# Expert products of 160 tokens in plain fp32, with 32 more tokens' expert dots taken from gathered rows

## The reference, cut to what matters

```python
top, pos = lax.top_k(cand, PEER_TOPK)            # per token and head: 16 of 16384 experts
idx = jnp.take_along_axis(cand_idx, pos, axis=-1)
g = jax.nn.softmax(top.astype(jnp.float32), axis=-1)
u = u_tab[idx]                                   # u_tab, v_tab: 16384 x 2048, 128 MB each
vv = v_tab[idx]
act = jax.nn.gelu(jnp.einsum('thkd,td->thk', u, hb), approximate=False) * g
return jnp.einsum('thk,thkd->td', act, vv)       # 8 heads x 16 picks per token
```

## Time and profile before

| | us |
|---|---|
| three runs: median (lowest to highest) | 1760.01 (1758.25 to 1761.03) |
| the profiled execution, span | 1758.1 |
| UP: first matmul to last matmul | 551.15 to 1159.68 |
| DOWN: first matmul | 1162.90 |
| POOL: first put, last gather of `u_tab` | 601.37, 1138.01 |

### The profile page before, as it was taken

The page is one execution under the profiler, slowest core; times in us unless marked ns, Lnnn a source line. Parts: engine busy times, 40 slices in busy tenths (PEclk is TensorE's granted clock), DMA queues, the critical chain, the costliest instruction groups (busy, mean ns, idle before and its releaser), DMA issues.

```text
span 1758.1 us, 28277 instructions
## 1 busy us (share of the span) xinstructions
PE 1732.3 (99%) x9480; PEld 1517.9 (86%) x9480; DVE 1535.3 (87%) x2469; ACT 799.5 (45%) x1185; POOL 603.1 (34%) x413
## 2 busy tenths in 40 slices
PE   7999999999999999999999999999999999999998
PEld 5888888644999999999999999988888888888886
DVE  4668899967688898998999999989999999999997
ACT  3001222300545555556555555554455544555454
POOL 1000000011000388788688888613321211112110
PEclk9999999999999999999999999999999999999999
DMA  9999986699798777987899999999999999999994
GB/s 380 421 421 422 424 322 252 234 387 417 301 349 272 219 218 223 296 253 224 249 382 389 399 411 404 401 365 411 414 413 410 390 404 398 397 399 389 407 387 190
DMA packets 142648, 617.22 MB, mean 351 GB/s; under 512 B 45347, under 2 KB 45939, under 8 KB 87411
## 3 DMA queue, kind: packets, MB, share of 16 engines
q1 hardware_dynamic: 80530, 410.04, 60.0%
q0 software_dynamic: 55712, 202.52, 31.9%
q10 hardware_dynamic: 6336, 3.75, 0.7%
HBM read 598.19 MB, written 16.89 MB: 350 GB/s over the span
## 4 chain that ended last, share of the span: by engine, by line
PE 76%; DMA 9%; DVE 8%; POOL 4%; issue 2%; ACT 1%; DVEq 0%; ACTq 0%; POOLq 0%; SPq 0%
PE ps L1448 33%; PE ps L1110 14%; PE ps L1117 9%; DMA raw<-in_w_ada 7%; PE ps L1161 5%; PE ps L1331 5%; POOL weights L570 3%; PE ps L1172 2%; DVE raw L1547 2%; PE ps L1103 2%; PE ps L1277 2%; DMA early<-in_w_front 1%; DVE w_low L1489 1%; DVE big L1603 1%; POOL big L555 1%
## 5 line engine op out<-in xcount | busy, mean ns | idle before, releaser
L805 ACT ACTIVATE w_hi<-raw 128x1024 fp32r<-128x1024 f32 x444 | 468.8, 1059 | 458.6 <-PE ps L1448 187.4
L1489 DVE TENSOR_TENSOR w_low<-raw,w_hi 128x1024 fp32r<-128x1024 f32 x444 | 541.5, 1224 | 85.5 <-ACT w_hi L805 77.6
L570 POOL DMA_INDIRECT weights<-sel x192 | 366.0, 1906 | 69.2 <-issue 57.6
L1110 PE MATMUL ps<-a,w_hi 128*128 128x384 f32 x1920 | 383.9, 341 | 0.8 <-issue 0.8
L1110 PEld LDWEIGHTS ps<-a,w_hi 128*128 128x128 f32 x1920 | 326.9, 189 | 1.6 <-issue 1.0
L1448 PE MATMUL ps<-w_low,a 128*128 128x512 f32 x1024 | 273.8, 389 | 0.0
L1448 PE MATMUL ps<-w_hi,a 128*128 128x512 f32 x1056 | 268.1, 389 | 1.5 <-ACT big L918 1.5
L1117 PEld LDWEIGHTS ps<-a,w_low 128*128 128x128 f32 x1920 | 247.1, 191 | 2.6 <-DVE w_low L1489 2.3
L1117 PE MATMUL ps<-a,w_low 128*128 128x192 f32 x1920 | 248.2, 271 | 0.7 <-DVE w_low L1489 0.6
L1448 PEld LDWEIGHTS ps<-w_hi,a 128*128 128x128 f32 x1056 | 198.2, 188 | 42.6 <-ACT big L918 1.6
L1448 PEld LDWEIGHTS ps<-w_low,a 128*128 128x128 f32 x1024 | 192.3, 188 | 39.8
(11 more groups left out here) (240 smaller groups left out, 2008.2 us busy)
## 6 DMA issues: line engine op xcount, KB each, us to landing
raw<-in_peer_u SPq DMA_DIRECT2D x128, 1024.0 KB
raw<-in_peer_v SPq DMA_DIRECT2D x256, 512.0 KB
early<-in_w_front SPq DMA_DIRECT2D x56, 1024.0 KB, 11.4
raw<-in_w_ada POOLq DMA_DIRECT2D x48, 1024.0 KB, 9.6
raw<-in_w_ada SPq DMA_DIRECT2D x32, 1024.0 KB
raw<-in_peer_wq SPq DMA_DIRECT2D x16, 1024.0 KB
big<-in_w_gate_f POOLq DMA_DIRECT2D x16, 1024.0 KB, 6.0
weights<-third SPq DMA_DIRECT2D x16, 768.0 KB, 19.1
```

Source lines behind the costliest of these rows:

```text
L570: gp.indirect_dma_start(weight_elements, bass.IndirectOffsetOnAxis(ap=put_at[:, c:c + 1], axis=0), put_gate[:, c:c + 1], None, compute_op= ...
L805: act.activation(high_at(ph, j), raw[:, s % RING, :], ACT.Copy).then_inc(hi_ready, 1)
L1110: done = pe.matmul(ps[:, b % 2, 0:2 * TD].rearrange("p (m t) -> p m t", m=2), high_at(ph, j)[:, k * P:(k + 1) * P], a_pair[:, kc, :, 0:TD] ...
L1489: dve.tensor_tensor(w_low[:, s % RING, :], raw[:, s % RING, :], high_at(ph, j).bitcast(F32), ALU.subtract).then_inc(lo_ready, 1)
```

## The change

UP multiplies tokens 0 to 159 (`TU`) only, in plain fp32, unsplit, for every block: 16 matmuls of 160 columns. `hi`, `lo`, the second sum and its add go from UP. Blocks use four PSUM banks. Tokens 160 to 191 get their dots from gathered rows: four tokens' picks share a gather (`QUARTERS`), so 32 "mid" gathers are added to the 50, all through the same three buffers, and each takes a whole 2048-wide dot on DVE against `h_mid`. Their gelu times gate goes into the weight matrix by 32 puts of its own (`put_mid`), in place of 32 of the old ones: 160 + 32 puts. In DOWN those tokens' columns of a weight group are copied, not multiplied. The routing is straight code: two routes, two dots, `pair_gates`, three dots per head. Each head's choices go out as ten small DMAs of ACT in place of four, at set blocks of UP. PE turns `h` twice, once more than before.

```diff
+TU = 160
 TD = 192
+TM = TD - TU
 TS = T - TD
 SLICES = P // TS
+QUARTERS = P // TM
...
+WHOLE = tuple(range(16))
+PH_UP = Phase(PH_WQ, EXPERT_BLOCKS // 32, 16, plain=WHOLE, groups=tuple(range(22, 30)))
...
+EARLY_ROWS = ROWS - LATE_STEPS
+MID_ROWS = PEER_HEADS * TOPK // QUARTERS
+HEAD_MID = MID_ROWS // PEER_HEADS
+ROW_ORDER = []
+for h in range(PEER_HEADS):
+    ROW_ORDER += [("mid", HEAD_MID * h + k) for k in range(HEAD_MID)] + [("end", n) for n in FIRST_OF_HEAD[h:h + 1]]
+ROW_ORDER += [("end", n) for n in range(EARLY_ROWS) if n not in FIRST_OF_HEAD]
+U_ROWS = len(ROW_ORDER)
...
+MID_HALF = MID_ROWS // 2
+MID_ACTS_AT, MID_PUT_FROM = (38, 50), 44
+MID_DONE = [ROW_ORDER.index(("mid", MID_HALF * (q + 1) - 1)) + 1 for q in range(2)]
...
+PUTS_SECOND, PUTS_FIRST = PEER_HEADS * TOPK // QUARTERS, PEER_HEADS * TOPK
-PUTS_UP = 52
-PUTS_BEHIND = [0, 0, 24, 0, 40] + [2, 2, 2, 2, 1] * 9
-PUTS_AT = [min(PUTS_UP + sum(PUTS_BEHIND[:n]), PUTS) for n in range(EARLY_ROWS + 1)]
-assert PUTS_AT[EARLY_ROWS] == PUTS
+PUT_ORDER = [(tt, h, k) for h in range(PEER_HEADS) for tt, picks in ((0, TOPK), (1, TOPK // QUARTERS)) for k in range(picks)]
+PUTS_BY = [min(PUTS, 9 * (n + 1) // 4) for n in range(U_ROWS)]
...
@@ SyncE @@
+                    sp.wait_ge(weights_put[2], 16 * MID_ROWS)
+                    sp.wait_ge(row_used, U_ROWS)
...
@@ GpSimd @@
-            for m in range(PUTS_UP):
-                put_weights(m)
+            def put_mid(n):
+
+                if n % MID_HALF == 0:
+                    gp.wait_ge(mid_made, n // MID_HALF + 1)
+                if n and n % HEAD_MID == 0:
+                    gp.wait_ge(weights_put[2], 16 * n)
+                gp.indirect_dma_start(weight_elements, bass.IndirectOffsetOnAxis(ap=mid_at[:, n:n + 1], axis=0),
+                                      mid_act[:, n:n + 1], None, compute_op=ALU.add).then_inc(weights_put[2], 16)
+
...
-            for n in range(EARLY_ROWS):
+            gp.dma_start(gate_cols, gate_saved[0, :].rearrange("(p a) -> p a", p=P)).then_inc(gate_f_saved, 16)
+            for n in range(U_ROWS):
+                kind, row = ROW_ORDER[n]
                 if ROW_NTH[n] > 1:
-                    gp.wait_ge(row_used, max(m for m in range(n) if ROW_BUF[m] == ROW_BUF[n]) + 1)
-                if n % HEAD_ROWS == 0:
-                    gp.wait_ge(row_info_in, 16 * SLICES * (n // HEAD_ROWS + 1))
-                gather(n, u_rows, (got[0], got[1], third[:, :])[ROW_BUF[n]], row_in[ROW_BUF[n]])
-                for m in range(PUTS_AT[n], PUTS_AT[n + 1]):
+                    gp.wait_ge(row_used, n - 2)
+                where = (got[0], got[1], third[:, :])[ROW_BUF[n]]
+                if kind == "mid":
+                    gp.wait_ge(mid_info_in, 16 * QUARTERS * (row // HEAD_MID + 1))
+                    gp.indirect_dma_start(where, None, u_rows, bass.IndirectOffsetOnAxis(ap=mid_ix[:, row:row + 1], axis=0))\
+                        .then_inc(row_in[ROW_BUF[n]], 16)
+                else:
+                    gp.wait_ge(row_info_in, 16 * SLICES * (row // HEAD_ROWS + 1))
+                    gather(row, u_rows, where, row_in[ROW_BUF[n]])
+                for m in range(PUTS_BY[n - 1] if n else 0, PUTS_BY[n]):
                     put_weights(m)
+                if 0 <= n - MID_PUT_FROM < MID_ROWS:
+                    put_mid(n - MID_PUT_FROM)
...
@@ ScalarE @@
+            def gelu(n):
+
+                act.wait_ge(split_used, PH_UP.s + 2 * (n + 1))
+                act.activation(routed_v[:, strip_of(n), 0:TU], ps[:, n % 4, 0:TU], ACT.Gelu).then_inc(gemm_evac, 1)
+            def pair_exp(b):
+
+                act.wait_ge(gate_in, 2 * b + 2)
+                heads = gates[:, 2 * b:2 * b + 2, :]
+                act.activation(heads, heads, ACT.Exp).then_inc(gate_exp, 1)
+
...
+            def pack_head(b):
+
+                act.wait_ge(picked_ready, 3 * b + 3)
+                for n in range(QUARTERS):
+                    k = TOPK // QUARTERS
+                    dst = mid_info[n * TM:(n + 1) * TM, :, k * b:k * (b + 1)]
+                    src = picked[TM:2 * TM, 3 * (n // 2):3 * (n // 2) + 3, b, n % 2 * k:(n % 2 + 1) * k]
+                    act.dma_start(dst, src).then_inc(mid_info_in, 16)
...
+                for n in range(QUARTERS):
+                    k = TOPK // QUARTERS
+                    dst = put[n * TM:(n + 1) * TM, :, k * b:k * (b + 1)]
+                    src = picked[0:TM, 3 * (n // 2):3 * (n // 2) + 2, b, n % 2 * k:(n % 2 + 1) * k]
+                    act.dma_start(dst, src).then_inc(put_in, 16)
+
+            def mid_gelus(q):
+
+                act.wait_ge(row_used, MID_DONE[q])
+                half = mid_dots[:, q * MID_HALF:(q + 1) * MID_HALF]
+                act.activation(half, half, ACT.Gelu).then_inc(mid_gelu, 1)
...
+            for n in range(EXPERT_BLOCKS):
+                if n == 5:
+                    act.wait_ge(ada_used, 2 * KC)
+                if n == 32:
+                    act.wait_ge(x2_saved, 16)
+                if n == 70:
+                    act.wait_ge(sel_ready, 2 * PEER_HEADS)
...
+                gelu(n)
+                if n == 0:
...
+                if n == 2:
+                    put_h_tok(h_mid, 0)
+                if n == 4:
+                    put_h_tok(h_tok, 1)
+                if n >= 6 and n % 7 == 6 and n // 7 < PEER_HEADS:
+                    pair_exp(n // 7)
+                if n >= 8 and n % 7 == 1 and n // 7 - 1 < PEER_HEADS:
+                    pack_head(n // 7 - 1)
+                if n >= 11 and n % 7 == 4 and n // 7 - 1 < PEER_HEADS:
+                    packed(n // 7 - 1)
+                if n in (58, 70):
+                    mid_gelus(n // 70)
...
@@ TensorE @@
-            def add_low(b, i, per):
-
-                pe.wait_ge(low_put, at(i, per, b - B_UP + 1))
-                pe.matmul(ps[:, b % 2, 0:TD], ident_r[:, :], low[:, :], start=False, stop=True,
-                          skip_group_check=True).then_inc(summed, 1)
-
-            def product(ph, n, i, ahead=None):
+            def product(ph, n, i, h, ahead=None):
 
                 b = ph.block + n
                 if i is None and b < B_UP + 2:
                     pe.wait_ge(gemm_evac, 10 + 2 * (b - B_UP))
+                elif i is None and b < B_UP + 4:
+                    pe.wait_ge(sc_copied, 8)
                 else:
-                    pe.wait_ge(gemm_evac, at(i, ph.blocks, b - 1))
+                    pe.wait_ge(gemm_evac, at(i, ph.blocks, b - 3))
+                pe.wait_ge(landed[b % 4], at(i, 16 * ph.blocks // 4, 16 * (b // 4 + 1)))
                 for half in range(2):
-                    if half and (b > B_UP or i is not None) and not by_vector(ph, n - 1, i):
-                        add_low(b - 1, i, ph.blocks)
                     if ahead:
-                        ahead(2 * n + half, i)
-                    s, j = ph.s + 2 * n + half, 2 * n + half
...
                     for k in range(UCH):
                         kc = half * UCH + k
-                        done = pe.matmul(ps[:, b % 2, 0:2 * TD].rearrange("p (m t) -> p m t", m=2),
-                                         high_at(ph, j)[:, k * P:(k + 1) * P], a_pair[:, kc, :, 0:TD], start=kc == 0,
-                                         stop=False, skip_group_check=True)
-                    done.then_inc(hi_used, 1)
-                    pe.wait_ge(lo_ready, ph.count(j, i))
-                    for k in range(UCH):
-                        kc = half * UCH + k
-                        done = pe.matmul(ps[:, b % 2, 0:TD], w_low[:, s % RING, k * P:(k + 1) * P], a_hi[:, kc, 0:TD],
-                                         start=False, stop=False, skip_group_check=True)
-
+                        done = pe.matmul(ps[:, b % 4, 0:TU], raw[:, s % RING, k * P:(k + 1) * P], h[:, kc, 0:TU],
+                                         start=kc == 0, stop=kc == KC - 1)
...
@@ VectorE @@
+            def row_dot(m):
+
+                kind, n = ROW_ORDER[m]
+                row = (got[0], got[1], third[:, :])[ROW_BUF[m]]
+                if m == 0:
+                    dve.wait_ge(h_tok_made, 8)
+                dve.wait_ge(row_in[ROW_BUF[m]], 16 * ROW_NTH[m])
+                h, dot = (h_mid, mid_dots) if kind == "mid" else (h_tok, dots)
+                dve.tensor_tensor_reduce(row, row, h, 1.0, 0.0, ALU.mult, ALU.add, dot[:, n:n + 1]).then_inc(row_used, 1)
+
+            def mid_acts(q):
+
+                half = slice(q * MID_HALF, (q + 1) * MID_HALF)
+                dve.wait_ge(mid_gelu, q + 1)
+                dve.tensor_tensor(mid_act[:, half], mid_dots[:, half], mid_gate[:, half], ALU.mult).then_inc(mid_made, 1)
+
+            for n in range(4):
+                gate_f_step(2 * KC - 4 + n)
+            dve.wait_ge(x2_saved, 16)
+            dve.wait_ge(zeros_made, 3)
+            rows_done = 0
+            for b in range(PEER_HEADS):
+                route(2 * b)
+                route(2 * b + 1)
+                for _ in range(2 if b else 0):
```

(52 more changed lines are left out.)

375 lines of the change are left out of this document (103 added, 272 removed).

## The result

The changed kernel takes 1814.34 us (median of 4, 1813.29 to 1815.96) and the one before 1759.13: a ratio of 1.0312, 95% interval 1.030 to 1.0325. The profiled execution has a span of 1814.2 us for 1758.1 before.

What follows compares the result with a forecast made beforehand. POOL bounds UP: from 603, 569 us of instructions and holds, then 10, 7 and 7 put the last dot at 1196; edge 6.7 and cold start 2 make DOWN 42 us later: span 1800, median 1802, range 1780 to 1822.

Steps and rivals of the forecast that it cites:

- PE: UP's plain products at 0.276 us each, 4.42 a block; alone they end at 1124, some 35 us earlier than before.
- the stalls: In the routing, a head takes 36 us against 30.9 of PE's blocks; PE falls 27 us behind, ending at about 1151.
- POOL's instructions: 192 puts and 82 gathers in UP, at the shortest prices and 0.30 between: 462 us.
- The holds: POOL waits in UP while two-input DVE instructions end: 76 dots at 1.3 us, 99, plus 8 for route steps.
- The waits for a buffer: POOL waits for a free gather buffer during UP's routing: 10 us over eight heads.
- The landing and the dot: At UP's end, the last gather's landing and its dot on DVE: 7 us.
- The edge: Between UP's last dot and DOWN's first matmul, the same steps as before: 6.7 us.
- The cold start of PE: DOWN's first matmuls after PE idles some 50 us: 2 us extra, within 0 to 4.
- DOWN: `make_group`'s product and copy add 5 us of DVE at most, covered by busy PE; counted as nothing.
- rival B: UP gains less or nothing: holds of 0.6 us each, last dot at 1139 or PE at 1151; 1745 to 1760; 9 in 100.
- Bytes: UP moves 220 million bytes, 536 us at 411 GB/s; a gather can land every 6 us, POOL is slower, so DMAs hide.
- rival A: Dots do not hold POOL in UP; PE ends UP at 1124 to 1151; time 1724 to 1751; 8 in 100.

Runs made afterwards that it cites:

- best2_narrow: Changed kernel with most dots' h in PSUM, puts reordered, ACT's exps and sends every eighth block, and half a row in each UP gather: 1715.95 us.
- best1: Changed kernel with 74 dots reading h from PSUM, three puts a row to row 38, then one, mid puts in fours from row 50: 1763.24 us.

## Why the prediction was right, and by how much it missed

Forecast 1802, measured 1814. The mechanism was the one forecast: slower, because POOL becomes the bound of UP, held by the longer dots. By its own steps, on the profiled execution (forecast span 1800, measured 1814.2):

- **PE** alone was forecast to end at 1124, and best2_narrow ends UP's products at 1115.5: they cost 0.272 us and not 0.276, and began 1.4 us earlier. With the stalls it was to end at 1151 and ended at 1149.2. That this is so near is luck: the stalls cost 33.7 us, where 27 were forecast. The time of the kernel does not hang on it.
- **The start of POOL's work**, 603: the first gather is at 602.70.
- **POOL's instructions** at the shortest prices, 462: from 602.70 to the end of the last gather at 1197.0 are 594.3, less 98.2 of holds and 39.0 idle, 457.1.
- **The holds**, 107 (76 dots at 1.3, so 99, and 8 by routes): 98.2. The dots' part was as forecast, 94.1 us in 73 instructions, 1.29 each. The routes held next to nothing: all instructions that began outside a dot share the other 4 us.
- **The waits for a buffer**, 10 in the routing: 35.0, the one large miss. Six times, once a head, POOL stood for 4.5 to 6.2 us at a mid gather for a buffer, and once, at 638.60, for 2.9 us for a head's choices. A head took DVE 37.5 us and not 36, and POOL's work for it was 27.3 + 40.7 / 7 = 33.1 and not 34.3. That leaves 4.4 us a head where 1.7 were counted. The last rows' 7 were 4.0. All this together: the last gather is over at 1197.0 in place of 1189. That these come to 8 only is luck in part, since others went against the waits: the waits 25 us too low, the instructions 5, the holds 9 and the last rows 3 too high.
- **The landing and the dot** of the last row, 7: 9.0 (1197.0 to 1205.97).
- **The edge**, 6.7: 7.5. **The cold start of PE**, 2 within 0 to 4: 2.9.
- **DOWN**, nothing: 2.6 (586.0 us from its first matmul to the end of its products in place of 580.5, less the 2.9); in the other runs it was 0 to 1.1; PE's weight loads waited 2.1 us here for `w_low`, three times; whether that belongs to the change wasn't settled.
- Sum of the misses: 8 + 2 + 0.8 + 0.9 + 2.6 = 14.3, and 1814.2 - 1800 is 14.2.

The other signs that it had named came too: the longest put of UP took 3.67 us (1.5 to 3.8 forecast), gathers 44 to 75 came every 8.2 us (8 to 9), and PE idled 62.7 us before DOWN (some 50). One range doesn't follow from its own steps: rival B's last dot at 1139 or PE at 1151 give 1743 or 1751, where it says 1745 to 1760.

What the prediction had not seen is in "Bytes": "So the DMAs hide". That is true only while POOL is slower. PE at full pace takes 1.05 MB in 4.42 us, 237 GB/s, which leaves 174 for a row in 6 us, and 43 rows are left at 887 (148 instructions, 105 of them puts). By this estimate they land by 887 + 258 = 1145 at the earliest, then come the last dot, 2.3, and the edge, 6.7: DOWN at 1154, a time of 1751. With the measured 0.272 us a product PE takes 241 GB/s and the same estimate gives some 1757. So with that routing no more than the upper end of rival A's 1724 to 1751 was to be had: it dropped the holds and forgot the bytes. With the holds gone the kernel was at 1772, and with the order mended at 1763. The change takes 44.3 us from PE (UP's last product ends at 1115.5 in best2_narrow and at 1159.8 before). It adds 32 rows of 1.05 MB, 34 MB, 82 us of the DMAs' time at 411 GB/s, to UP, where the DMAs run full from 900 on as soon as the holds are gone (412 GB/s in best1 at 900 to 1000, 381 in the changed kernel).

## What to carry to other kernels

A DMA issued by POOL is an instruction of POOL. Count these with their holds, and let the DVE instructions beside them have one operand in PSUM, or make them short. When work goes from PE to gathers, price it in POOL's instructions and in bytes, both, before the time that PE saves; and when a bound is taken away, work out the next one before the gain is counted. An idle wait taken out of an engine's order comes back if what fills it could have run later but its neighbour could not.
